# Splitting the first projection of a diffusion step in two halves of its depth, and giving one expert's weights a place of their own

## The reference, cut to what matters

```
mod = silu(cond) @ w_ada + b_ada                 # w_ada 1024 x 6144; sh1, sc1 are its first 2048 columns
h   = rmsnorm(x, g_norm1) * (1 + sc1) + sh1
u   = h @ w_in                                   # 1024 x 7168: b, c, v, x_r, g, m_a, m_b
x_c = conv4(x_r)                                 # depthwise, 4 taps, along the tokens
r, i = sigmoid(x_c @ w_gate_a + b), sigmoid(x_c @ w_gate_x + b)     # 8 heads, 2 directions
...                                              # scans, short convolution, merge, w_o
for e in range(32):                              # after the router, top 2 of 32
    y += gate[e] * ((silu(t @ w1[e]) * (t @ w3[e])) @ w2[e])        # 1024x512, 1024x512, 512x1024
```

## Time and profile before

| | us |
|---|---|
| runs | 949.2, 949.86, 952.07 (median 949.86) |
| profiled execution | 951.76 |
| its span, first to last instruction | 949.7 |
| TensorE busy in the span | 885.1 (93%) |
| VectorE, ScalarE, GpSimd busy | 571.0, 282.9, 333.4 |
| mean DMA rate over the span | 301 GB/s |

### The profile page before, as it was taken

The page is one execution under the profiler, slowest core; times in us unless marked ns, Lnnn a source line. Parts: engine busy times, 40 slices in busy tenths (PEclk is TensorE's granted clock), DMA queues, the critical chain, the costliest instruction groups (busy, mean ns, idle before and its releaser), DMA issues.

```text
span 949.7 us, 12700 instructions
## 1 busy us (share of the span) xinstructions
PE 885.1 (93%) x4502; PEld 551.9 (58%) x4502; DVE 571.0 (60%) x990; ACT 282.9 (30%) x499; POOL 333.4 (35%) x301
## 2 busy tenths in 40 slices
PE   3899999999999999999999999998988988989895
PEld 1579988989999999755444344333333333433331
DVE  2489984677102342236477777775766666766677
ACT  4366374645334332021321121121212121211112
POOL 0046946556556646122222232231313131313100
PEclk9999999999999999999999999999999999999998
DMA  9962556464572537637699999999999999999992
GB/s 344 356 256 89 184 178 220 162 240 172 183 263 91 187 120 250 240 158 291 240 393 411 410 411 419 414 416 402 409 394 415 396 403 389 406 404 408 402 419 87
DMA packets 61882, 285.70 MB, mean 301 GB/s; under 512 B 6895, under 2 KB 11279, under 8 KB 47492
## 3 DMA queue, kind: packets, MB, share of 16 engines
q1 hardware_dynamic: 58228, 278.63, 75.9%
q0 software_dynamic: 2480, 3.11, 1.1%
q10 hardware_dynamic: 1120, 3.24, 0.9%
HBM read 286.80 MB, written 3.19 MB: 305 GB/s over the span
## 4 chain that ended last, share of the span: by engine, by line
PE 65%; DMA 26%; DVE 3%; SPq 2%; ACT 2%; issue 1%; DVEq 0%; ACTq 0%; POOL 0%
DMA ring<-in_w 13%; DMA slot<-in_w 11%; PE bank L889 10%; PE bank L890 10%; PE bank L893 10%; PE bank L1113 9%; PE bank L1130 7%; PE bank L959 4%; PE bank L1114 3%; DMA ring<-in_w_ada 2%; PE bank L1090 2%; PE bank L825 2%; PE bank L903 2%; PE bank L1068 1%; SPq L637 1%
## 5 line engine op out<-in xcount | busy, mean ns | idle before, releaser
L478 POOL TENSOR_TENSOR subs<-ring,subs 128x512 fp32r<-128x512 f32 x138 | 205.5, 1514 | 176.5 <-ACT subs L1262 176.5
L889 PE MATMUL bank<-h_hl,subs 128*128 128x384 f32 x488 | 165.9, 340 | 0.6 <-ACT lru L1340 0.6
L890 PE MATMUL bank<-h_hl,subs 128*128 128x384 f32 x488 | 164.1, 336 | 0.0
L1113 PE MATMUL bank<-ring,x_T 128*64 128x512 f32 x256 | 116.7, 597 | 11.7 <-DMA slot<-in_w 4.3
L1114 PE MATMUL bank<-ring,x_T 128*64 128x512 f32 x256 | 117.1, 598 | 0.0
L2079 DVE TENSOR_TENSOR hg<-hg,lru 128x512 f32<-128x512 f32 x186 | 116.7, 680 | 0.0
L676 POOL COPY idx<-lists 64x1 uint32 (+1 forms) x31 | 5.5, 179 | 297.3 <-PE bank L1068 292.8
L1113 PE MATMUL bank<-slot,x_T 128*64 128x512 f32 x192 | 89.2, 606 | 11.5 <-DMA slot<-in_w 8.2
L1262 ACT ACTIVATE subs<-ring 128x1024 fp32r<-128x1024 f32 x72 | 76.1, 1060 | 72.6 <-PE bank L893 72.6
L889 PEld LDWEIGHTS bank<-h_hl,subs 128*128 128x128 f32 x488 | 91.7, 188 | 5.8 <-issue 4.2
L893 PE MATMUL bank<-h_hl,subs 128*128 128x384 f32 x488 | 94.7, 336 | 0.0
(11 more groups left out here) (249 smaller groups left out, 1504.2 us busy)
## 6 DMA issues: line engine op xcount, KB each, us to landing
ring<-in_w SPq DMA_DIRECT2D x40, 2048.0 KB, 29.2
slot<-in_w SPq DMA_DIRECT2D x30, 2048.0 KB, 29.0
ring<-in_w_in SPq DMA_DIRECT2D x14, 2048.0 KB, 8.0
ring<-in_w_ada SPq DMA_DIRECT2D x12, 2048.0 KB, 8.9
gate_w<-in_w SPq DMA_DIRECT2D x10, 2048.0 KB, 30.0
ring<-in_w SPq DMA_DIRECT2D x16, 1024.0 KB, 31.0
slot<-in_w SPq DMA_DIRECT2D x12, 1024.0 KB, 31.7
ring<-in_w_rnn_out SPq DMA_DIRECT2D x2, 2048.0 KB, 8.3
```

Source lines behind the costliest of these rows:

```text
L478: last = eng.tensor_tensor(pair[:, 1, ks], src[:, ks], pair[:, 0, ks].bitcast(F32), ALU.subtract)
L889: eng.matmul(ps[:, 0:T], pair[:, 0, k, :], x[:, 1, k, :], start=(k == 0), stop=False)
L890: eng.matmul(ps[:, 0:T], pair[:, 0, k, :], x[:, 0, k, :], start=False, stop=False)
L1113: eng.matmul(ps[HALF:P, :], x_T[:, k, :], w1_k[:, k, :], start=(k == 0), stop=(k == KD - 1))
```

## The change

The first chunks come in the order ada 0, ada 2, xr, ada 1, ada 3. As soon as ada 0 and 2 are there, shift and scale of the first four of eight depth blocks are known; the first projection runs over that half for all four quarters (`high_parts`, `low_parts`), with the rows and columns of ada 1 and 3 put between its matmuls, and then over the other half. The weights' quarters are split in half quarters for this (`half_quarter`): eight pieces of 128x512, six of which fit in `subs`, so the last two wait until the first half's are used (`half_used`). All eight low parts are GpSimd's. The conditioning vector's silu comes ahead of the norm's root on ScalarE, and the parameters' copy ahead of the norm on VectorE. Two constant matmuls stand behind the first `ada_rows`; the six of the start before are gone. The gates of heads 0 and 1 come after xr tiles 4 to 7.

For the experts, w3 of expert 2 (`APART`) is loaded once into four pieces of buffers that are free by then (1 MB, 0.5 MB and twice 0.25 MB), after the last normalisation (`h2_ready`) and the last router product. All later loads stand one place earlier in the round of eight, so w2 of expert 2 no longer waits for expert 0, and the loads of experts 3 and 4 are issued as soon as expert 0 and 1 are through.

```diff
-    W_IN = [("xr", 0), 0, ("xr", 1), ("c", 0), ("v", 0), 1, ...
+    W_IN = [("xr", 0), ("xr", 1), 0, ("c", 0), ("v", 0), 1, ...
-    START = [("par", 0), ("par", 1), ("adaR", 0), ("xT", 0), ("xT", 1), ("xT", 2), ("xT", 3), ("adaR", 1),
-             ("adaC", 0), ("xT", 4), ("xT", 5), ("xT", 6), ("xT", 7), ("adaR", 2), ("adaC", 1),
-             ("adaC", 2), ("adaR", 3), ("adaC", 3)]
-    chunks += [("ada", j) for j in range(4)]
+    START = [("par", 0), ("par", 1), ("adaR", 0)] + [("xT", k) for k in range(KD)] + \
+        [("adaR", 2), ("adaC", 0), ("adaC", 2)]
+    stream += START + [("adaR", 1), ("adaC", 1), ("adaR", 3), ("adaC", 3)]
+    chunks += [("ada", 0), ("ada", 2), ("xr", 0), ("ada", 1), ("ada", 3)]
...
         def moe_slot(i, s, w):
+            c = 3 * s + w
+            if isinstance(i, int) and i == 0 and c < 3 * APART[0] + APART[1]:
+                return c
+            return (c - 1) % MSLOTS
...
-            load(2, 2, 1)
-            multiplied_in(0)
             load(2, 2, 2)
+            eng.wait_ge(h2_ready, TT)
+            wait_tile(eng, ("route", TT - 1))
+            for piece, k0 in zip(apart, apart_at):
+                src = w3_v[2][:, k0 * CW:(k0 + piece.shape[1]) * CW].rearrange("p (k n) -> p k n", n=CW)
+                eng.dma_start(piece, src).then_inc(apart_landed, 16)
+            for s in (3, 4):
+                multiplied_in(s - 3)
+                load(s, s, 0)
+                load(s, s, 1)
+                multiplied_out(s - 3)
+                load(s, s, 2)
...
# GpSimd
-            for q in range(SUBS, NQ):
-                write_lo(eng, q, lo_p)
+            eng.wait_ge(h_ready, CT)
+            for r in range(2 * CT):
+                write_half_lo(eng, r)
+            for q in range(CT, NQ):
+                write_lo(eng, q)
...
# TensorE, first_project
+                for k in range(K2):
+                    if k == K2 - 1:
+                        ada_rows(1)
+                    high_parts(k)
+                low_parts(0)
+                ada_columns(1)
+                low_parts(1)
+                ada_rows(3)
+                low_parts(2)
+                low_parts(3).then_inc(half_used, 1)
+                ada_columns(3)
+                for k in range(K2, KD):
+                    high_parts(k)
+                for m in range(CT):
+                    low_parts(CT + m).then_inc(tile_done, 1)
...
# TensorE, the start
             for name, number in START:
-                if (name, number) == ("adaC", 3):
-                    constants(spare, 1)
                 start_work[name](number)
-                if (name, number) == ("adaC", 2):
-                    constants(spare, 1)
-            constants(spare, 4)
+                if (name, number) == ("adaR", 0):
+                    constants(spare, 2)
...
# ScalarE, after the last squares
-            eng.wait_ge(mean_ready, 1)
-            eng.activation(stat[:, 0, 2, :], stat[:, 0, 1, :], ACT.Sqrt).then_inc(rms_ready, 1)
             wait_read(eng, ("par", 0))
             wait_read(eng, ("par", 1))
             eng.wait_ge(cvec_zero, 1)
             eng.activation(cvec[:, :, 0:2], pT[:, CCTX:CCTX + 2 * KD].rearrange("p (c k) -> p k c", c=2),
                            ACT.Silu).then_inc(cvec_ready, 1)
+            eng.wait_ge(mean_ready, 1)
+            eng.activation(stat[:, 0, 2, :], stat[:, 0, 1, :], ACT.Sqrt).then_inc(rms_ready, 1)
...
+            ada_copy(0)
+            for k in range(KD):
+                copy_xT(k)
+            ada_copy(2)
+            half_hi(0)
...
-            copy_xr(2)
-            copy_xr(3)
+            for h in range(2, KD):
+                copy_xr(h)
             gate_sigmoids(0)
             gate_exps(0)
-            copy_xr(4)
-            copy_xr(5)
+            copy_c(0, range(0, 3))
             gate_roots(0)
-            copy_xr(6)
-            copy_xr(7)
-            copy_c(0)
+            copy_c(0, range(3, CT))
...
# VectorE
+            for half in range(2):
+                ks = range(CT * half, CT * (half + 1))
+                for j in (half, 2 + half):
+                    ada_columns(j)
...
             conv_rnn(0)
             conv_rnn(1)
             decay_rates()
-            conv_rnn(2)
-            conv_rnn(3)
+            for h in range(2, KD):
+                conv_rnn(h)
             gate_inputs(0)
-            for h in range(4, KD):
-                conv_rnn(h)
             scans(0)
```

More of the change, by code:

```diff
@@ L137, in layer_program @@
         else:
-            add_chunk(*item)
+            if item == ("xr", 0):
+                stream += [("xr", m) for m in range(CT)]
+            else:
+                add_chunk(*item)
             if item in ADA_AFTER:
@@ L466, in wait_split, with write_lo, write_half_lo @@
         def wait_split(eng, q):
[L468 to L473, removed]
+            eng.wait_ge(lo_p, q + CT + 1)
+        def write_lo(eng, q):
             src, pair = quarter(q)
[L476 removed]
+            eng.wait_ge(hi_ready, q + CT + 1)
             for ks in (slice(0, KD // 2), slice(KD // 2, KD)):
                 last = eng.tensor_tensor(pair[:, 1, ks], src[:, ks], pair[:, 0, ks].bitcast(F32), ALU.subtract)
[L479 removed]
+            last.then_inc(lo_p, 1)
+        def write_half_lo(eng, r):
+            src, pair = half_quarter(r)
+            eng.wait_ge(hi_ready, r + 1)
+            eng.tensor_tensor(pair[:, 1], src, pair[:, 0].bitcast(F32), ALU.subtract).then_inc(lo_p, 1)
         def wait_chunk(eng, n):
@@ L620, in load_expert @@
                 load(e, s, 2)
-            for s in range(3, LAP):
+            for s in range(5, LAP):
                 load_expert(s, s)
@@ L858, in router_constants, with first_project, high_parts @@
                 mm.then_inc(tile_done, 1)
[L860 to L864, removed]
+            def first_project(x):
+                K2 = KD // 2
+                def high_parts(k):
                     eng.wait_ge(h_ready, k + 1)
-                    for m in range(SUBS):
+                    for m in range(CT):
+                        r = CT * (k // K2) + m
@@ L867, in first_project @@
                         if k == 0:
[L868 to L876, removed]
@@ L877, in first_project @@
-                project(kind, 0, x, range(SUBS, CT))
+                            open_tile(("xr", m))
+                        if k % K2 == 0:
+                            eng.wait_ge(hi_ready, r + 1)
+                        ps, pair = bank[N_OF[("xr", m)] % BANKS], half_quarter(r)[1]
+                        eng.matmul(ps[:, 0:T], pair[:, 0, k % K2, :], x[:, 1, k, :], start=(k == 0), stop=False)
+                        eng.matmul(ps[:, 0:T], pair[:, 0, k % K2, :], x[:, 0, k, :], start=False, stop=False)
@@ new lines, in low_parts @@
+                def low_parts(r):
+                    ps, pair = bank[N_OF[("xr", r % CT)] % BANKS], half_quarter(r)[1]
+                    eng.wait_ge(lo_p, r + 1)
+                    for j in range(K2):
+                        k = K2 * (r // CT) + j
+                        mm = eng.matmul(ps[:, 0:T], pair[:, 1, j, :], x[:, 0, k, :], start=False, stop=(k == KD - 1))
+                    return mm
+                for k in range(K2):
+                    if k == K2 - 1:
+                        ada_rows(1)
+                    high_parts(k)
@@ L1366, in gate_roots, with copy_c @@
                 eng.activation(r_f, r_f, ACT.Sqrt).then_inc(root_done, 1)
-            def copy_c(half):
-                for m in range(CT):
+            def copy_c(half, ms=range(CT)):
+                for m in ms:
                     ps, free = tile(("c", CT * half + m))
@@ L1679, in norm2_gain @@
                         .then_inc(gain_ready, 1)
-            for j in range(4):
-                ada_columns(j)
-            for j in range(4):
-                wait_read(eng, ("adaC", j))
-            for cnd in range(2):
-                last = eng.scalar_tensor_tensor(out=A1[:, :, cnd], in0=mod[:, KD:2 * KD, cnd], scalar=1.0,
-                                                in1=pT[:, GN1:GN1 + KD], op0=ALU.add, op1=ALU.mult)
-            then(last)
             def split_lo(x_hl, x, k, count, done):
```

157 lines of the change are left out of this document (101 added, 56 removed).

## The result

The changed kernel takes 954.25 us (median of 13 runs, 951.9 to 962.0) beside 949.86 (13 runs, 948.2 to 952.1) for the kernel before, measured in turn on the same chip: a ratio of 1.0065, 95% interval 1.0046 to 1.0083. It is 0.65% slower; the forecast was 945.8, between 940 and 951.5. The profiled execution took 952.64 us, its span is 950.9 (before 951.76 and 949.7).

The account below looks back on a forecast made before the run. Two clocks in series bound the kernel: TensorE until the first expert has run, then the DMA engines. Front 0.1 plus ninth place 4.0 made 4.1 us, so 945.8 against 949.86, range 940 to 951.5.

Parts of the forecast that it names:

- From the four tiles to the c projection: Stretch after the first four projection tiles: TensorE stands 3.8 us instead of 2.1, 1.7 us lost.
- The chain of copies and convolutions: ScalarE's copies and VectorE's convolutions of heads 0 to 5 ahead of the first sigmoid: TensorE restarts at X + 26.2.
- X: End of the first four projection tiles, forecast at 56.1 us (bounds 53.4 and 59.5), 1.8 us earlier than before.
- the first rival: All of the front arrives, without clock falls or VectorE meeting GpSimd, and the place's full load: 11.7 us, 938.2; chance 0.13.
- The start: Up to the end of the first four tiles: line 1699 starts 10.0 us earlier, the tiles end 1.8 us earlier.
- VectorE beside GpSimd: First projection's second half: the two take turns, GpSimd's low parts delaying VectorE's blocks; bounds 0 and 2.8, taken 0.7 us.
- The floor of 53.4: End of the first four tiles before the clock and VectorE-beside-GpSimd costs: 53.4 us against 57.93, 4.5 us earlier.
- The ninth place: Expert stage: a 2.10 MB load fits for nothing into the DMA hole from 456 to 462 us; gain taken 4.0 us.
- the engines would run dry: Expert stage, DMA engines after 504.3 us: empty for about 1.1 us, at most 2.3, or not at all.
- the slower one: Rival: VectorE's convolutions become the bound as GpSimd never rests beside heads 2 to 5; 957.3 us, chance 0.12.
- the front gives back what the place brings: Rival: two clock falls and full turn-taking, X = 59.5, 1.6 + 1.7 lost, 4.0 won: 949.2 us; chance 0.22.
- h: Time of one convolution head; TensorE stands 4h - 9.1 us, and from 5.0 the kernel is slower by over 0.3%.

Follow-up runs that it names:

- the front alone: The changed kernel without the ninth place, its expert-stage edits taken back to the eight places of before: 957.8 us, 1.0089 against the kernel before.
- the order alone: The kernel before, old start, with only the first gates behind both xr quarters and ScalarE's and VectorE's orders as the change has them: 955.97 us, 1.0072.
- the run with the constants in the changed kernel: The changed kernel with constant matmuls in three of TensorE's holes of the start (three, four, three): 951.43 us, 1.0019 against the kernel before.
- The constants on the old start: The kernel before with the changed gate order alone, plus constant products in TensorE's three holes at xr7 and the last two gate tiles: 953.46 us, 1.0043.
- the old gates: The changed kernel with the gates of heads 0 and 1 back between xr tiles 3 and 4, ScalarE's and VectorE's orders as before: 947.12 us, 0.9980.
- with the wait: The kernel before with the ninth place alone, SyncE issuing its four pieces only once the last rows of h_rows are written to DRAM: 944.62 us, 0.9951.
- the place alone: The kernel before with only the ninth place, SyncE's and TensorE's edits in the expert stage; the start is untouched: 947.93 us, 0.9982.

## Why the prediction was wrong

The failed step is "From the four tiles to the c projection": 1.7 us lost by the forecast, 6.0 measured, on the old start and in the changed kernel alike (c's last tile ends 5.1 and 8.0 later than before, the four tiles 0.8 earlier and 2.0 later). Two terms of that step failed: in the changed kernel the chain that c waits for was 2.8 us longer than summed, and the clock behind the wait, put at nothing, cost 1.5 there and up to 2.8 in other runs.

- *The chain of copies and convolutions* sets when c starts, as forecast, but took longer. Heads 0 and 1 end at X + 4.5 (forecast 4.4). The decay rates took 6.6 instead of 5.3: three of their small instructions took 1.2 to 1.3 us beside GpSimd, where 0.16 to 0.18 is what they take without it. Heads 3 to 5 took 3.4, 5.1 and 3.4, 11.9 instead of 10.5. So the first c tile came at X + 29.0 instead of X + 26.2; before it was X + 24.5.
- *Which waits there are* was incomplete. I had TensorE arrive at X + 22.4 and stand once, for a sigmoid. But quarter 7 is fed behind copy 4, and that copy waits for head 2's convolution, behind the decay rates: xr7 itself stood 2.7 us for its weights. All waits together are 5.1 (2.69, 0.49, 1.92), not 3.8. This changed where TensorE stands and not when c starts, which the chain sets.
- *What a wait costs* was the error of kind. I priced the clock in the start only and gave the waits here no price beyond their length. Behind the last of them the clock fell: nine products of the first c tile at 0.32 instead of 0.173 us made it 1.5 longer in the changed kernel, some seventeen made it 2.6 to 2.8 longer in the front alone and in the order alone. The fall behind xr7 took another 1.4 of TensorE's time, but that was waited out (the run with the constants in the changed kernel). The constants on the old start show this half by itself: 1.0072 to 1.0043.

One bound of this step was also summed wrongly: three short heads of 2.45 leave 0.65 us of waiting by the prediction's own terms, so 1.5 won and not 2.1, and the first rival is 938.8 instead of 938.2. It decides nothing.

The start was mis-sized too: X = 59.97 in the changed kernel's profile instead of 56.1, beyond the bound of 59.5; in two other executions with the same start (the front alone, the old gates) it was 57.55 and 58.06, inside it.
- The clock fell in both holes. From 27.7 to 33.9 and from 49.1 to 54.3 us TensorE worked at 1.2 GHz; at twice the time for each product that costs somewhat under half of the 6.2 and 5.2 us, about 2.9 and 2.4, 5.3 together against 2.0 taken and 3.3 as the bound. My bound came from the one fall of before, 3.3 us long; in the three executions these lasted 2.7 to 6.2, and how long differs from run to run of the same code. Nor was the fall of before a fixed part of its start: the profiles of the place alone and of the order alone, with that same start, show none before 80 us. The first fall followed the columns and a hole of 2.6 us without a fall ahead of it. The Trainium skill (TensorE: Matmul & The Clock Gate, "What's actually happening") has the clock follow how busy the engine has been; I said that this would count the holes alone. With constants in the holes behind the same columns no fall came, in three runs: for these two falls the holes decided, which fits the Trainium skill better than my own reading. The holes are not the whole of it: in the profile of before the clock also fell near 341 us, behind 32 products of 36 columns and without a hole, and no run here settles why.

```profile
337.57 4.04 PE L856 MATMUL bank<-wr,mod 128*128 128x36 f32 x32
```

- VectorE beside GpSimd: the gain and the first block took 0.94 + 2.08 us at 45.35 instead of the 0.24 + 1.25 of the first half, 1.5 more against 0.7 taken; a later pair took 2.65 instead of 0.66, just while GpSimd worked (49.99 to 52.51). The Trainium skill (SBUF — State Buffer, "SBUF: two separate sides") calls the port that the two share a lock held for an instruction, not a split; the small instructions of 1.2 us, about one of GpSimd's 1.24, agree.
- The floor of 53.4 "without extra costs" was too low: 56.1, 57.2 and 57.35 in the three executions with the clock up. The old start ended at 57.1 in two executions without a fall. Of the 4.5 us that I gave this start at most 1 is there to be had.

The ninth place was right in size (4.0; 4.7 with the wait) and wrong in "for nothing". The engines' hole from 456 to 462 was filled, but it was not free: the write of the rows and the gather of expert 1 used it to get through in time. Only 1.7 us came through by itself. That the engines would run dry for 1 to 2 us is not shown: from 475 to 608 us they move 410 GB/s before, 408 with the place and its wait, and 398 with the place alone, where the late gather held up the loads.

Of the rivals, the slower one (957.3) had the right side and in number was nearest; "the front gives back what the place brings" (949.2), with its two falls, was 5 below. The slower one's mechanism, a chain of convolutions for which TensorE stands, was there, but not its size: h was 3.6 on average of heads 2 to 5, below the 5.0 from which it was to decide, and by its formula that makes 3.0 us of loss. The rest came through the clock, which its formula left out, and through the start and the gather. The clock alone would not have made slower likely: the forecast's own wait, priced with 1.5 to 2.8 us behind it, gives 947.3 to 948.6.

Of the signs that I named, these held: line 1795 (1699 before) near 26, one fall from 25 to 32, the filled hole, weight waits of 22.7 against 24. These failed: the first gate at X + 21.0 against X + 16.8, 1.9 us of waiting for sigmoids against 4, c's end at 107 against 99. Of the ways to be wrong, the second half of the first projection stood 4.1 us, under the 5 named; one head of convolutions took 5.1, just over 5; the DMA rate moved by 1.5% from 475 to 608 us (404 against 410) and by 0.5% from 475 to 900 (404 against 406).

## What to carry to other kernels

Price a wait of TensorE with what follows it: here most waits of 1.9 to 4.1 us were followed by a half clock that cost 1.3 to 2.9 us, and a few useless products in the hole, in a bank that is free anyway, took that part back. It counts only where nothing later is waited for: a half clock ahead of another wait was waited out. When a block of work moves behind another one, follow every queue that feeds the block in front: the new first wait was for weights whose feeding had been tied to a copy two chains away. An idle stretch of the DMA engines may be what lets a small write and a gather through in time; before it is filled with a large load, ask which small transfer has to land there, and issue the load behind it.

## What the runs showed of the hardware

- A gather of 64 rows lands in 2.6 us at best and 8.6 in the middle of the expert stage (issue to landing, least and median of 31). What decided was its lead over the expert loads: 3.8 us ahead (before, and with the wait) and 1.6 ahead (old gates) nobody waited; 0.9 ahead TensorE waited 1.3 us, 0.5 ahead 4.1 us.
- A 512 KB write to DRAM with 2 MB of loads issued beside it landed after 8.9 to 10 us (five runs); with those loads behind it it was there within 4.8 us (two runs), and without them after 4.8 to 6.2 us.
- A fall of the clock after a hole lasted 2.7 to 6.2 us of work, at nearly twice the time for every product (0.32 against 0.173 us), and differed in length between executions of the same code; seven constant products in the two holes of 2.6 and 4.1 us were enough that none came, in three runs.
- One VectorE instruction of 16 columns took 1.26 us when it ran beside GpSimd's subtractions; in the kernel before, without them, the same one took 0.16.
